# One-core transformer trunk on Trainium2: first loads, filler products, unit order and 32-row spreads rearranged

## The reference, cut to what matters

```python
hn = rms_norm(h_res, attn_norm[layer])
r_q, r_k, r_v, r_g, c_q, c_kv, k_rope = jnp.split(hn @ w_in[layer], IN_SPLITS, axis=-1)
...
y_ret = from_heads(head_rms(retention(rq, rk, rv))) * ret_out_gain[layer] * jax.nn.silu(r_g)
y_mla = from_heads(head_rms(latent_attention(c_q, c_kv, k_rope, ...))) * mla_out_gain[layer]
h_res = h_res + jnp.concatenate([y_ret, y_mla], axis=-1) @ w_out[layer]
hn = rms_norm(h_res, ffn_norm[layer])
h_res = h_res + (swiglu(hn, ...) if layer % 2 == 0 else moe_swiglu(hn, ...))
```

## Time and profile before

| | |
|---|---|
| median of 3 runs | 1539.18 us (1536.52 to 1541.78) |
| the profiled execution | 1540.51 us, its span 1538.5 us |
| TensorE, weight load, VectorE, ScalarE busy | 1513.2, 1305.5, 1233.3, 1013.4 us |
| first attention layer, up to the dense entry | 0 to 155 us |
| second attention layer | the same steps as in the first, about 400 us later |

### The profile page before, as it was taken

The page is one execution under the profiler, slowest core; times in us unless marked ns, Lnnn a source line. Parts: engine busy times, 40 slices in busy tenths (PEclk is TensorE's granted clock), DMA queues, the critical chain, the costliest instruction groups (busy, mean ns, idle before and its releaser), DMA issues.

```text
span 1538.5 us, 21849 instructions
## 1 busy us (share of the span) xinstructions
PE 1513.2 (98%) x8362; PEld 1305.5 (85%) x8362; DVE 1233.3 (80%) x1068; ACT 1013.4 (66%) x946; POOL 38.0 (2%) x42
## 2 busy tenths in 40 slices
PE   9999999999999999999999999999999999999997
PEld 9779999999987888888888888888888888888885
DVE  6746776767884568889898888888888888888887
ACT  7655434334574557777777777777777777777775
POOL 0000000000000012000000000000000000000000
PEclk9999999999999999999999999999999999999998
DMA  9314454444324349999999999989999999999992
GB/s 355 134 46 170 159 181 189 178 170 188 117 110 164 137 154 386 393 366 402 373 349 403 377 349 401 386 344 395 391 350 386 391 371 364 397 378 348 422 377 95
DMA packets 64707, 447.91 MB, mean 291 GB/s; under 512 B 8121, under 2 KB 8153, under 8 KB 12432
## 3 DMA queue, kind: packets, MB, share of 16 engines
q1 hardware_dynamic: 61200, 437.49, 72.7%
q0 software_dynamic: 3456, 9.71, 2.2%
HBM read 442.20 MB, written 7.36 MB: 292 GB/s over the span
## 4 chain that ended last, share of the span: by engine, by line
PE 89%; DVE 6%; ACT 4%; issue 1%; ACTq 0%; DVEq 0%; POOL 0%; POOLq 0%
PE bank L501 86%; PE bank L505 3%; DVE w_lo L1240 1%; DVE w_lo L1559 1%; ACT w_hi L1157 1%; ACT w_hi L939 1%; DVE scratch L1298 0%; ACT scratch L1013 0%; ACT scratch L1141 0%; ACT scratch L1014 0%; DVE scratch L1283 0%; DVE r_row L1267 0%; DVE scratch L1287 0%; DVE parts L1254 0%; DVE scratch L1294 0%
## 5 line engine op out<-in xcount | busy, mean ns | idle before, releaser
L501 PE MATMUL bank<-w_hi,parts 128*128 128x512 f32 x2688 | 834.5, 392 | 3.1 <-DVE parts L1543 1.5
L1559 DVE TENSOR_TENSOR w_lo<-ring,w_hi 128x2048 fp32r<-128x2048 f32 x288 | 659.4, 2292 | 93.5 <-ACT w_hi L1157 90.1
L1157 ACT ACTIVATE w_hi<-ring 128x2048 fp32r<-128x2048 f32 x288 | 551.9, 1919 | 173.4 <-PE bank L501 146.0
L501 PEld LDWEIGHTS bank<-w_hi,parts 128*128 128x128 f32 x2688 | 499.7, 188 | 107.7 <-DVE w_lo L1559 4.9
L501 PE MATMUL bank<-w_lo,parts 128*128 128x512 f32 x1344 | 523.8, 390 | 0.0
L501 PE MATMUL bank<-parts,w_hi 128*128 128x272 f32 (+1 forms) x2240 | 432.5, 291 | 3.2 <-DVE parts L1254 1.8
L501 PEld LDWEIGHTS bank<-parts,w_hi 128*128 128x128 f32 x2240 | 354.5, 189 | 4.7 <-DVE w_lo L1240 2.0
L501 PE MATMUL bank<-parts,w_lo 128*128 128x272 f32 (+1 forms) x1120 | 323.0, 288 | 0.0
L501 PEld LDWEIGHTS bank<-w_lo,parts 128*128 128x128 f32 x1344 | 252.2, 188 | 53.3
L501 PEld LDWEIGHTS bank<-parts,w_lo 128*128 128x128 f32 x1120 | 212.4, 190 | 0.4
L1240 DVE TENSOR_TENSOR w_lo<-ring,w_hi 128x2048 fp32r<-128x2048 f32 x71 | 161.3, 2288 | 53.6 <-ACT w_hi L939 53.6
(11 more groups left out here) (180 smaller groups left out, 636.3 us busy)
## 6 DMA issues: line engine op xcount, KB each, us to landing
ring<-stream SPq DMA_DIRECT2D x359, 1024.0 KB, 5.5
hT<-stream SPq DMA_DIRECT2D x48, 1024.0 KB
ring<-stream SPq DMA_DIRECT2D x4, 512.0 KB, 6.9
ring<-stream SPq DMA_DIRECT2D x2, 976.0 KB, 4.7
ring<-stream SPq DMA_DIRECT2D x2, 768.0 KB, 10.1
c_sb<-consts SPq DMA_DIRECT2D x1, 1136.0 KB, 11.8
hT<-h SPq DMA_DIRECT2D x2, 544.0 KB, 5.5
ring<-stream SPq DMA_DIRECT2D x2, 544.0 KB
```

What stands on the lines that cost most here:

```text
L501: return release(nc.tensor.matmul(dst, lhsT, rhs, start=start, stop=stop), inc)
L1157: A(w_hi[:, n % HSLOTS, :], moe_slot(m), ACT.Copy).then_inc(split_hi, 1)
L1559: V.tensor_tensor(w_lo[:, n % HSLOTS, :], moe_slot(m), w_hi[:, n % HSLOTS, :].bitcast(F32), ALU.subtract).then_inc(split_lo, 1)
```

## The change

Seven edits. (1) Rows are loaded in four pieces instead of two, with both halves of unit 0 a step earlier, and the two splitting engines take unit 0's half first. (2) 24 filler products instead of 48. (3) The second gate unit and the first table change places (units 11 and 12); the product `g2`, `g3` and the weights follow. (4) `prob_transposes(0)` stands ahead of the turns `rv`. (5) `high(b+8)` and `low(b+8)` move from among the rotations to behind the value copies, and between two masks. (6) `spread` multiplies only the 32 rows of its head, and `bM0` to `bM3` stand in a row ahead of `yR3`. (7) At the dense entry `low(b+15)` moves behind the rows' low parts and `row_scale(1)` ahead of the next `low`.

```diff
-U_UQ, U_UKV, U_RV, U_RG, U_T1, U_T2, U_WO = 6, 7, 8, 10, 12, 13, 14
+U_UQ, U_UKV, U_RV, U_RG, U_T1, U_RG2, U_T2, U_WO = 6, 7, 8, 10, 11, 12, 13, 14
...
-            for half in range(2):
-                c = slice(half * UNIT // 2, (half + 1) * UNIT // 2)
-                sp.dma_start(hT[:, 4 * half:4 * half + 4, :], h0[:, 4 * half:4 * half + 4, :]).then_inc(x_in[half], 16)
-                sp.dma_start(ring[:, 0, c], stream[0, :, c]).then_inc(slot_in[0] if half else first_in, 16)
+            def load_rows(q):
+                sp.dma_start(hT[:, 2 * q:2 * q + 2, :], h0[:, 2 * q:2 * q + 2, :]).then_inc(x_in[q], 16)
+
+            def load_half(j):
+                c = slice(j * UNIT // 2, (j + 1) * UNIT // 2)
+                sp.dma_start(ring[:, 0, c], stream[0, :, c]).then_inc(slot_in[0] if j else first_in, 16)
+
+            load_half(0)
+            load_rows(0)
+            load_rows(1)
+            load_half(1)
+            load_rows(2)
+            load_rows(3)
...
-                    mm(dst, col(C_ROW + h * P), sq3[:, 2 * odd, :], True, True, out_done)
+                    q = slice(32 * h, 32 * h + 32)
+                    mm(dst, col(C_ROW + h * P)[q, :], sq3[q, 2 * odd, :], True, True, out_done)
...
+                prob_transposes(0)
                 for t in range(3):
...
-                prob_transposes(0)
                 proj("g0", U_RG, 0)
...
-                weigh("yR3", 7, rv)
                 spread("bM2")
                 spread("bM3")
-                proj("g3", U_RG + 1, 1)
+                weigh("yR3", 7, rv)
+                proj("g3", U_RG2, 1)
...
-            keep_clock(48)
+            keep_clock(24)
...
-                    if name in ("q1", "q3", "k1", "k3"):
-                        high(b + 5 + ["q1", "q3", "k1", "k3"].index(name))
+                    if name in ("q1", "q3", "k1"):
+                        high(b + 5 + ["q1", "q3", "k1"].index(name))
...
                     keep(f"v{t}", vm[0:rows, t, :], rows, 512)
+                high(b + 8)
                 exps(0)
...
+            high_half(0)
             for k in range(DK):
+                if k == 4:
+                    high_half(1)
                 row_high(0, k)
-                if k % 4 == 3:
-                    high_half(k // 4)
...
                 rope(7)
-                low(b + 8)
...
                     mask_max(h)
+                    if h == 1:
+                        low(b + 8)
...
                     if layer == 0 and d == 6:
-                        low(b + 15)
                         row_low(1, 3)
                         row_low(1, 4)
...
                     row_low(1, 7)
+                    low(b + 15)
                     sum_squares(1)
...
-                        if c == 0:
-                            row_scale(1)
...
             attention(0)
+            row_scale(1)
             low(SPLIT_OF[DENSE_AT] + 2)
             dense()
```

More of the change, by code:

```diff
@@ L98 @@
          "qn0", "qn1", "qpe0", "qn2", "qpe1", "qn3", "kn0", "kn1", "kn2", "kn3", "v0", "v1", "v2",
[2 rows of a table removed]
+         "rT0", "rT1", "rT2", "rT3", "rv0", "rv1", "rv2", "g0", "yM0", "g1", "yM1", "g2", "yM2", "yM3", "yR0", "sM", "yR1", "yR2", "bM0", "bM1", "bM2", "bM3",
+         "yR3", "g3", "sR", "bR0", "bR1", "bR2", "bR3"])
 N_OUTS = len(OUTS)
@@ L260, in build @@
         const_in, fn_in, out_stored = sem("const_in"), sem("fn_in"), sem("out_stored")
-        x_in, gains_in, rw_in = [sem("x_in0"), sem("x_in1")], sem("gains_in"), sem("rw_in")
+        x_in, gains_in, rw_in = [sem(f"x_in{q}") for q in range(4)], sem("gains_in"), sem("rw_in")
         round_shifted = sem("round_shifted")
@@ L697, in attention @@
                 weigh("yM1", 1, vm)
-                proj("g2", U_RG + 1, 0)
+                proj("g2", U_RG2, 0)
                 prob_transposes(3)
@@ L950, in row_high @@
                     act.wait_ge(h_added, [0, 0, 8 + DK * (CHUNKS - 1)][n] + k + 1)
-                elif k % 4 == 0:
-                    act.wait_ge(x_in[k // 4], 16)
+                elif k % 2 == 0:
+                    act.wait_ge(x_in[k // 2], 16)
                 if n == 1 and k == 4:
@@ L1582, in _ @@
             dve.wait_ge(gains_in, 16)
+            low_half(0)
             for k in range(DK):
+                if k == 4:
+                    low_half(1)
                 row_low(0, k)
-                if k % 4 == 3:
-                    low_half(k // 4)
             low(1)
@@ L1686 @@
             units[at + U_RV + i] = cols(rv[:, 256 * i:256 * (i + 1)])
-            units[at + U_RG + i] = cols(rg[:, 256 * i:256 * (i + 1)])
+            units[at + (U_RG, U_RG2)[i]] = cols(rg[:, 256 * i:256 * (i + 1)])
         uq = x["w_uq"][layer].reshape(QR, HEADS, P + ROPE)
```

## The result

The changed kernel took **1532.03 us** (median of 6 runs, 1530.06 to 1533.26), the kernel before, on the same chip, 1539.83 (median of 6 runs, 1536.52 to 1542.16). The ratio is 0.995, 95% interval 0.9936 to 0.9965: faster by 5.4 to 9.9 us, 7.8 between the medians. The forecast was 1531.3 and a difference of 7.85. The total came out; several of its terms did not, and they cancelled. The profiled execution took 1530.65 us, its span 1528.8.

What follows compares the result with a forecast made beforehand. TensorE, busy 98% of the span, was taken as the bound, so only its gaps could gain. 0.9 + 0.35 + 1.2 + 1.7 + 3.7 = 7.85 us took 1539.18 to 1531.3, range 1528 to 1537.

Steps and rivals of the forecast that it cites:

- The start: First loads, filler and row order, once: an earlier TensorE gains 0.9 us, from waits of 0.62 and 0.26.
- the landing of unit 2 is not moved: First loads: unit 2 arrives when it did, so an earlier TensorE can give only the 0.62 us wait.
- the fifth rival: First loads give nothing because unit 2 is late: 1532.2 us, within the forecast's own range; no separate chance given.
- Half clock behind the 2 us gap: First loads: half clock in TensorE's 2.3 us gap would cost nothing, since cq0 must be done only by 22.5.
- Unit 8's split: Both attention layers: splitting unit 8 later, off the rows ahead of query copies and rotations, gains 0.35 us in both.
- Tables: Both layers, mask table loaded ahead of the second gate unit: VectorE's 6.38 us wait goes, nothing gained, nothing lost.
- Transposes: Both layers, first head's probability transposes ahead of the value turns: fill a 0.58 us TensorE wait, 1.2 us together.
- Spreads: Both layers, 32-row spreads in rows of four: partial overlap saves 0.86 us a layer, 1.7 together.
- an excursion of 0.29: Output spreads: going to a smaller row tiling and back costs 0.29 us, leaving 0.4 of the group's 0.69.
- the third rival: Spreads overlap fully: 1.64 us a layer, 3.3 in place of 1.7, ending at 1529.7; chance 0.10.
- The dense entry: Entry of the dense part, once: no 1.84 us wait or half clock, second gate product 3.7 us sooner; largest term.
- The second rival: Clock falls in the new 1.4 us gap where the dense part begins: 1.7 us less gain, 1533.0; chance 0.14.

## Why the prediction was right, point by point

**The start: 0.9 forecast, 0.2 at most found.** The failing step is "the landing of unit 2 is not moved". Over nine executions with the new order of loads unit 2 was split from 18.31 to 19.32 us, 18.95 in the mean; over three with the old one at 18.52, 18.61 and 18.88, 18.67 in the mean. The other half, TensorE's lateness, is real but varies: 0.62, 0.90 and, with the start put back, nothing. The two nearly cancel: the reciprocal starts at 23.96 in the mean of the nine and at 24.15 in that of the three, 0.2 us apart within a scatter of 1.1. That is the fifth rival, which the prediction named with its cause, in size; three executions against nine don't settle whether the 0.28 us of the landing is the order's doing or scatter. Half clock behind the 2 us gap cost nothing, as said: the root doesn't wait for TensorE.

**Unit 8's split: 0.35 forecast, 0.3 found.** Reciprocal to keys took 36.73 and 36.72 before and 36.34 to 36.55 in the twelve executions of changed kernels. In layer 1 the corresponding row of the table shows nothing (290.92, then 290.98). This edit was not undone alone.

**Tables: 0, and 0.** The 6.38 us wait of VectorE for the load is gone (its wait before the first mask, at 67.34, is 5.16 us and for TensorE), and no wait for a weight unit took its place ahead of the output product. Argued from the trace; not undone alone.

**Transposes: 1.2 forecast, 1.5 found** (0.76 a layer). The wait of 0.58 is the mechanism. Nearly all of the other 0.18 is a matter of reading: the wait in brackets counts from the end of the pass before, which the profile puts 0.29 us behind its start, while passes here start every 0.13 us when nothing holds them. From start to start the wait is 0.87 us (85.86 to 86.73) in place of 0.13, so 0.74 us are lost. The other waits of TensorE in this document are to be read the same way, some 0.16 us longer than in their brackets.

**Spreads: 1.7 forecast, 3.2 found.** Output group 0.96 a layer up to the next product and 1.07 and 1.02 by the rows around it, instead of 0.4; latent group 0.53 with all that lies beside it (1.29 less 0.76, and 69.71 less 69.18 with the spreads undone) instead of 0.46. The mis-sized term is the output group: I let only neighbours overlap and charged an excursion of 0.29. All four first passes start together, though; the second passes begin at

```profile
130.37 0.41 PE L510 MATMUL bank<-sq,c_sb 32*128 32x272 f32 x4
```

0.33 us behind them, and the group of eight passes lasts 0.67. That is the third rival's mechanism (1.38 less 0.29 is 1.09, found 0.96 to 1.07; 0.55, found 0.53), to which I gave 0.10. The Trainium skill (TensorE: Matmul & The Clock Gate, Part 3) had said that products in distinct 32-row groups run concurrently; the trace agrees, 0.67 us for what took 1.63. The row I leaned on instead, that 64 rows take as long as 128, was about products in the same rows, and the kernel with all spreads on rows 0 to 31 shows that this says nothing on different ones.

**The dense entry: 3.7 forecast, 3.7 found, for a reason that is half right.** 4.80 less the 1.07 of the spreads. Of it 1.80 is the reciprocal ahead of the split, shown by undoing it. 0.44 is the earlier split of the rows, shown likewise, and twice. The remaining 1.5 is the half clock: 7.6 us for 6.1 us of work in both executions of the kernel before. (At the second gate product, which the forecast was about, it is 39.14 less 34.63 less 1.07, 3.4.) I had tied the half clock to the gap of 1.84 us. But the changed kernel with that gap put back kept its clock twice. So the gap alone does not bring the fall; what decides it stays open. It may be something else in the changed kernel (the stretch ahead of the gap differs by the spreads). It may be chance too, with two executions on each side: behind the moment at which the filler sped up, the gap began 147.9 and 147.2 us later in the two that fell, and 145.9 and 146.3 us later in the two that did not. That the 1.5 us is a gain of this edit is therefore not shown; that no changed kernel had a fall there, in twelve executions, is. The second rival, a fall in the new gap of 1.38 us, did not happen in any of the ten executions without the old gap.

**Not in the sum at all: 1.5 us in layer 1, and not shown to be any edit's.** From the output spreads to the router product the changed kernel takes 2.54 us less, of which the spreads are 1.02. The rest is the clock. The same 4 us in the kernel before (router product at 556.57) and in the changed one (router product at 546.74):

```profile
552.00:556.00 4.00, 4.00 (x27) 4.00 (x25) 0.00 (x0) 3.02 (x6) 0.00 (x0) 0.67 0.00 0
```

```profile
552.00:556.00 4.00, 4.00 (x25) 3.99 (x25) 3.69 (x13) 0.77 (x3) 1.55 (x3) 0.63 0.86 315
```

In the first it lies ahead of the router product, where TensorE works without a gap; in the second behind it, where TensorE has waits of its own (1.12 and 1.58 us). But this is not how the changed kernel always runs. With the reciprocal put back, an edit that touches nothing of layer 1, the fall lies ahead of the router product, and the way there is 25.03 us instead of 23.41:

```profile
544.00:548.00 4.00, 4.00 (x26) 4.00 (x25) 0.00 (x0) 3.19 (x7) 0.00 (x0) 0.70 0.00 0
```

With late constants and the old order it is 24.98, and the kernel with 64 rows a spread has its fall there too. So three of twelve executions of changed kernels pay for it, and both of the kernel before. Why it comes at about this time in all of them is open.

**The sum.** 0.2 + 0.3 + 1.5 + 3.2 + 3.7 is 8.9 us, and 10.4 with the 1.5 of layer 1; the two first executions differ by 9.7, the second ones by 12.8, the timed runs by 5.4 to 9.9. Of the 10.4, 3.0 are two falls of the clock, at the dense entry and in layer 1, which both executions of the kernel before had. The changed kernels had falls as well, at other places. In the eleven executions that leave out no head's factor, from 0 to 3 falls that cost time lie ahead of the router product, 0.8 in the mean. Counted at 1.5 us each, about 1.8 of the 3.0 is a gain on average, and the sum is 9.2, inside what was timed. The difference to 7.8 no row settles: of executions without a profile only the mean clock is known, not where it fell. The prediction's 7.85 lies so close to 7.8 partly by luck. The start gave 0.7 less than forecast and the spreads 1.5 more, the others nearly what was forecast, and the timed runs show less than the path does.

## What to carry to other kernels

Products that use few rows are worth giving rows of their own and putting side by side: four took 0.67 us here instead of 1.63, and fewer rows without different ones made it worse. Before earning time at the start of a program, see how much the landing of a load differs between executions; here 1.0 us of scatter buried every reordering. And measure an edit by the distance between two instructions around it, repeated within 0.2 us here where no fall of the clock lies between, since whole times of the same kernel lie 3 us apart.

## What the runs showed of the hardware that I had not expected

**Falls of the clock wander, and where they land decides their price.** Stretches of 4 us with a granted clock under 1.00, ahead of the last 20 us: before, 152 to 160, 548 to 556 and 560 to 568; before again, 156 to 160, 552 to 556 and 568 to 576; changed, 16 to 24 and 548 to 556; changed again, 16 to 24, 60 to 64 and 552 to 556; start put back, 548 to 556 alone, which is the shortest span of all, 1525.1 us. One fall costs 1.5 to 1.6 us where TensorE works without a gap, and nothing at 16 to 24 us, where it waits for loads anyway. It needs no gap ahead of it either: in the kernel before TensorE was busy all of the time from 532 to 556 us, and the granted clock there went from 1.00 (532 to 548) to 0.50 (552 to 554). That the last products run at full clock, 3.70 us instead of 6.24 for the same eight passes, was so in three of twelve executions of changed kernels and in neither of the kernel before.

**The filler at the start runs at half speed first, for a time that differs by execution.** Its passes start 0.21 us apart, and from one pass on 0.11 us apart. That step came between 4.0 and 7.2 us in the fourteen executions: at 5.1 in the profiled execution of before, at 6.4 in the second, at 4.0 with the start put back. From 4 to 6 us TensorE worked on 15, 12 and 20 passes in these three, from 2 to 4 us on 11 in each. So 48 products took 12.31 to 13.48 us, and 24 took 6.98 to 8.47 in eleven executions. That it is the clock's rise from half to full is a reading of mine: the rate doubles, and the trace has no reading of the clock ahead of that moment (the windows print 1.00 there).

**Spreads in the same 32 rows are slower than in 128**: 2.02 us for the eight passes against 1.63.
